# Head norm of the differential attention moved from ScalarE and VectorE to GpSimd, with a reciprocal root by Newton steps

## What is computed

```python
def diff_attention(q, k, v, lam):          # 8 heads, head width 2 * 64 = 128
    s = einsum("bqhmd,bkhmd->bhmqk", qi, k) * d ** -0.5
    p = softmax(s, axis=-1)
    a = p[:, :, 0] - lam * p[:, :, 1]
    return einsum("bhqk,bkhe->bqhe", a, v)

def rms_norm(x, g):
    return x * rsqrt(mean(x * x, axis=-1) + EPS) * g

def diff_output(o, subln_g, lam_init, w_out):
    o = rms_norm(o, subln_g) * (1.0 - lam_init)   # over the 128 values of a head
    return o.reshape(B, L, D_MODEL) @ w_out
```

## Time and profile before

| | us |
|---|---|
| median of three timed runs | 4042.5 (4040.92 to 4044.31) |
| the profiled execution, its own time | 4037.7 |
| its span, first to last instruction | 4035.9 |

### The profile page before, as it was taken

One profiled execution on the slowest core, in us unless ns is written; L12 is line 12 of the kernel. 1 busy time (PEld: TensorE's weight loads), 2 busy tenths in 40 slices (PEclk: granted clock), 3 DMA queues, 4 the chain that ended last, 5 costly groups with the idle time before them and its releaser, 6 DMA issues.

```text
span 4035.9 us, 52710 instructions
## 1 busy us (share of the span) xinstructions
PE 3755.6 (93%) x22128; PEld 2863.9 (71%) x22128; DVE 1688.5 (42%) x4142; ACT 809.4 (20%) x1872; POOL 195.6 (5%) x271
## 2 busy tenths in 40 slices
PE   6978999889997999999997999889989799999996
PEld 2435545554444999999994554777764699999996
DVE  5442002474524544444423320777752554444442
ACT  1103000121002111111112000666640211111112
POOL 0000000000000000000000000000000000000001
PEclk9998999989997999999998999999999799999998
DMA  8651011222232788888871110100011388888886
GB/s 326 242 196 62 21 48 56 82 102 104 85 134 97 258 285 284 286 284 283 284 270 64 36 42 21 45 17 17 9 74 68 118 277 284 285 282 284 285 280 220
DMA packets 280302, 655.47 MB, mean 162 GB/s; under 512 B 8808, under 2 KB 9185, under 8 KB 276802
## 3 DMA queue, kind: packets, MB, share of 16 engines
q1 hardware_dynamic: 245202, 517.05, 35.6%
q0 software_dynamic: 34864, 135.05, 10.8%
HBM read 588.76 MB, written 57.02 MB: 160 GB/s over the span
## 4 chain that ended last, share of the span: by engine, by line
PE 86%; DVE 5%; ACT 5%; DMA 2%; issue 1%; SPq 0%; POOL 0%; DVEq 0%; ACTq 0%; POOLq 0%
PE ps L1075 25%; PE ps L784 14%; PE ps L1101 12%; PE ps L956 6%; PE ps L787 6%; PE ps L753 3%; PE ps L1151 3%; PE ps L891 3%; PE ps L907 3%; PE ps L1201 2%; PE ps L1170 2%; ACT hT L1454 1%; ACT hT L1268 1%; PE ps L1106 1%; PE ps L705 1%
## 5 line engine op out<-in xcount | busy, mean ns | idle before, releaser
L1075 PE MATMUL ps<-big,ring 128*128 128x144 f32 x8192 | 1031.7, 288 | 4.2 <-DVE big L1920 4.2
L1075 PEld LDWEIGHTS ps<-big,ring 128*128 128x128 f32 x8192 | 1014.6, 191 | 13.1 <-issue 11.8
L784 PE MATMUL ps<-hT,ring 128*128 128x384 f32 x1728 | 562.3, 489 | 6.2 <-issue 6.2
L1101 PE MATMUL ps<-big,ring 128*128 128x144 f32 x4096 | 512.0, 286 | 0.0
L1101 PEld LDWEIGHTS ps<-big,ring 128*128 128x128 f32 x4096 | 505.6, 190 | 0.0
L784 PEld LDWEIGHTS ps<-hT,ring 128*128 128x128 f32 x1728 | 330.6, 191 | 237.3 <-issue 11.4
L1948 DVE TENSOR_TENSOR big<-big,ps 128x144 f32<-128x144 f32 x256 | 77.8, 304 | 502.7 <-ACT big L1398 499.3
L1398 ACT ACTIVATE big<-ps 128x144 f32<-128x144 f32 x256 | 74.3, 290 | 980.5 <-PE ps L1075 980.5
L956 PE MATMUL ps<-ring,yT 128*128 128x512 f32 x576 | 247.5, 592 | 0.0
L787 PE MATMUL ps<-ring,hT 128*128 128x512 f32 x576 | 247.5, 592 | 0.0
L1988 DVE TENSOR_REDUCE gst<-ps 128x1 f32<-128x1152 f32 x144 | 173.2, 1232 | 149.5 <-PE ps L1155 149.3
(11 more groups left out here) (343 smaller groups left out, 3839.4 us busy)
## 6 DMA issues: line engine op xcount, KB each, us to landing
ring<-in_moe_wg SPq DMA_DIRECT2D x64, 2048.0 KB, 10.4
ring<-in_moe_wu SPq DMA_DIRECT2D x64, 2048.0 KB, 13.9
ring<-in_moe_wd SPq DMA_DIRECT2D x64, 2048.0 KB, 11.3
ring<-in_w_mod SPq DMA_DIRECT2D x24, 2048.0 KB, 12.3
big<-aff_t POOLq DMA_DIRECT2D x30, 512.0 KB, 3.9
ring<-in_w_in_even SPq DMA_DIRECT2D x7, 2048.0 KB, 7.8
ring<-in_w_in_odd SPq DMA_DIRECT2D x6, 2048.0 KB, 10.0
big<-x_res POOLq DMA_DIRECT2D x24, 512.0 KB, 8.0
```

Source lines behind the costliest of these rows:

```text
L784: i = mm(ps[:, b + g, 0:384], w[:, k, c * P:(c + 1) * P], hTv[:, k, g * 384:(g + 1) * 384], start=k == 0, stop=k == DK - 1)
L1075: last_mm = mm(ps[:, 3 + f % 2, g * CAP:(g + 1) * CAP], w[u - n0][:, k, c * P:(c + 1) * P], xsT[b][:, k, :], start=k == 0, stop=k == DK - 1)
L1101: last_mm = mm(ps[:, 3 + d % 2, 0:CAP], w[4 + d // 4][:, k, (d % 4) * P:(d % 4 + 1) * P], hid[:, k, :], start=k == 0, stop=k == DK - 1)
```

## The change

The root and the scaling go to GpSimd. At q == 8 VectorE still makes the mean square, and then a first guess for the reciprocal root by shifting its bits right by one (into `gstf[:, 60:69]`); it signals `a.var` after that. GpSimd waits for `a.var`, finishes the guess with one instruction (multiply by -1, add a constant, on the bits taken as integers), makes four Newton steps of four instructions each on nine columns, and multiplies the head's 128x1152 values by the result. All 17 small instructions go through a `Chain`, each waiting for the one before. The norm of head h - 2 stands behind `swap_halves(h)` in GpSimd's queue; the last two heads' norms follow. The Sqrt on ScalarE (`deviations`) and `norm_head` on VectorE are gone. VectorE waits for the previous head's `a.on` before it overwrites the columns.

```diff
--- before.py
+++ after.py
@@ -136,7 +136,7 @@
                    "e.cbev": ("e.act_ctx", 0), "e.cxev": ("e.act_ctx", 4), "e.c0ev": ("e.act_ctx", 9),
                    "e.c1ev": ("e.act_ctx", 12), "e.coh": ("e.dve_ctx", 0), "e.xctx": ("e.dve_ctx", 2),
                    "a.kt": ("r.kt", T), "a.s": ("r.stmm", 16), "a.t": ("r.sc", T), "a.pv": ("h.x", 10),
-                   "a.ckT": ("r.ktev", T), "a.tev": ("r.oev", T), "a.e": ("h.vtev", 2 * T), "a.std": ("r.std", 1),
+                   "a.ckT": ("r.ktev", T), "a.tev": ("r.oev", T), "a.e": ("h.vtev", 2 * T),
                    "a.nm": ("r.sm", T), "a.a": ("r.qf", 8), "a.oev": ("r.on", T), "a.var": ("r.var", 1)}
 
         def common(name):
@@ -648,8 +648,27 @@
             pool.wait_ge(*at("q.ev", 34))
             pool.dma_start(out[4][0, 0].rearrange("t h d -> t (h d)"), va[:, 8, :]).then_inc(s("out"), 16)
             pool.wait_ge(*at("a.kctx_out", 16))
+            def norm_head(ch, h):
+
+                pool.wait_ge(*at("a.var", h + 1))
+                x, y, w = gstf[:, 48:57], gstf[:, 60:69], gstf[:, 72:81]
+                tt = nc.gpsimd.tensor_tensor
+                ch(nc.gpsimd.tensor_scalar(y.bitcast(I32), y.bitcast(I32), -1.0, float(0x5f3759df), ALU.mult, ALU.add))
+                for _ in range(4):
+                    ch(tt(w, y, y, ALU.mult))
+                    ch(tt(w, w, x, ALU.mult))
+                    ch(nc.gpsimd.tensor_scalar(w, w, -0.5, 1.5, ALU.mult, ALU.add))
+                    ch(tt(y, w, y, ALU.mult))
+                r = y.rearrange("p (t o) -> p t o", o=1).to_broadcast([P, T, P])
+                tt(ohs[h % 2], ohs[h % 2], r, ALU.mult).then_inc(s("a.on"), 1)
+                pool.wait_ge(*at("a.on", h + 1))
+
+            roots = Chain(pool, "pool.roots")
             for h in range(2, AH):
                 swap_halves(h)
+                norm_head(roots, h - 2)
+            for h in (AH - 2, AH - 1):
+                norm_head(roots, h)
             after_mixer(1)
             experts(1)
             ld(misc[:, 0:1024].rearrange("p (o d) -> p o d", o=1),
@@ -1461,10 +1480,6 @@
                         act.wait_ge(*at("a.t", before + g + 1))
                         A(dst(512 * g, w), ps[:, 6 + g % 2, 0:w], ACT.Copy, **kw).then_inc(s("a.tev"), 1)
 
-                def deviations(h):
-                    act.wait_ge(*at("a.var", h + 1))
-                    A(gstf[:, 48:57], gstf[:, 48:57], ACT.Sqrt).then_inc(s("a.std"), 1)
-
                 exps(0)
                 act.wait_ge(*at("a.kctx_out", 16))
                 exps(1)
@@ -1474,14 +1489,11 @@
                         act.wait_ge(*at("a.pv", n))
                     evacuate(lambda o, w: aT[:, o:o + w], done, 9 if q < 8 else 1)
                     done = tev_of[n]
-                    if q == head_step - 1 and h:
-                        deviations(h - 1)
                     if n + 2 < len(steps):
                         exps(n + 2)
                     if q == head_step and h:
                         evacuate(lambda o, w: yTv[:, h - 1, o:o + w], done, 9, scale=lamc[:, 6:7])
                         done = head_tev[h - 1]
-                deviations(AH - 1)
                 evacuate(lambda o, w: yTv[:, AH - 1, o:o + w], done, 9, scale=lamc[:, 6:7])
 
 
@@ -1988,13 +2000,6 @@
                         nc.vector.tensor_reduce(gstf[:, c + 2 + m:c + 3 + m], bank(3 * m, 3)[:, 0:w], AX.X, ALU.max,
                                                 negate=True).then_inc(s("a.nm"), 1)
 
-                def norm_head(h):
-                    dve.wait_ge(*at("a.std", h + 1))
-                    ch(rec(gstf[:, 60:69], gstf[:, 48:57]))
-                    r = gstf[:, 60:69].rearrange("p (t o) -> p t o", o=1).to_broadcast([P, T, P])
-                    tt(ohs[h % 2], ohs[h % 2], r, ALU.mult).then_inc(s("a.on"), 1)
-                    dve.wait_ge(*at("a.on", h + 1))
-
                 def mix(n):
 
                     w = NT if steps[n][1] < 8 else P
@@ -2014,8 +2019,6 @@
                         mix(n + 1)
                     if n + 2 < len(steps):
                         maxima(n + 2)
-                    if q == head_step - 1 and h:
-                        norm_head(h - 1)
                     dve.wait_ge(*at("a.pv", n + 1))
                     if q == 0 and h >= 2:
                         dve.wait_ge(*at("a.tev", head_tev[h - 2]))
@@ -2025,9 +2028,12 @@
                     dve.wait_ge(*at("a.oev", n + 1))
                     ch(stt(junk2, o[:, q, :], 1.0, o[:, q, :], ALU.mult, ALU.mult, accum_out=gstf[:, 36 + q:37 + q]))
                     if q == 8:
-                        ts(gstf[:, 48:57], gstf[:, 36:45], 1.0 / P, EPS, ALU.mult, ALU.add).then_inc(s("a.var"), 1)
+                        if h:
+                            dve.wait_ge(*at("a.on", h))
+                        ch(ts(gstf[:, 48:57], gstf[:, 36:45], 1.0 / P, EPS, ALU.mult, ALU.add))
+                        ts(gstf[:, 60:69].bitcast(I32), gstf[:, 48:57].bitcast(I32), 1, None, ALU.arith_shift_right
+                           ).then_inc(s("a.var"), 1)
                         dve.wait_ge(*at("a.var", h + 1))
-                norm_head(AH - 1)
                 dve.wait_ge(*at("a.on", AH))
                 dve.sem_inc(s("m1.big_free"), 1)
```

## The result

The changed kernel takes 4030.66 us (median of 10 runs, 4023.73 to 4036.69), the kernel before 4041.71 us (10 runs, 4036.71 to 4047.1): 11 us less, a ratio of 0.997 with a 95% interval of 0.996 to 0.9979. The forecast was 4033.4, or 9.1 us less.

What follows compares the result with a forecast made beforehand. TensorE was taken to bound the attention. ScalarE's stall gone (-22.2), a longer tail (+6.1) and VectorE waiting beside GpSimd (+7.0) gave -9.1 us, so 4042.5 would fall to 4033.4 us; range 4023 to 4050.

Steps and rivals of the forecast that it cites:

- ScalarE's stall: Heads 1 to 7, q = 0 to 2: without Sqrt and table loads the steps fall to 5.85 us, gaining 22.2 us.
- more than four head ends with a low clock: Head ends in the attention: a sign that would show the prediction wrong; no size given.
- 18.0 if clock drops only move elsewhere: Lower bound of the gain from ScalarE's removed table loads, 7 x 2.57 us, against 22.2 booked.
- VectorE's scaling "by itself worth nothing": VectorE at q = 1: its scaling lies inside ScalarE's stall, so removing it alone gains nothing.
- GpSimd's chain: Per head on GpSimd: 17 small instructions at 0.3 us, 5.1 us, then the scaling at 2.7 us.
- The slack to q = 2: Between heads: the norm is done 8.3 us after L2028 starts, leaving 10 us of slack, so no cost.
- R3: Rival, chance 0.07: at 1.1 us a link GpSimd misses the date of q = 2; +20.5 us, 4063.
- R4: Rival, chance 0.06: another wait at q = 1 replaces ScalarE's, only the tail is left; +6.1 us, 4048.6.
- The tail: Last head's norm, with nothing beside it: 8.3 us where it took 2.18, so 6.1 us more.
- VectorE beside a working GpSimd: Attention, heads' ends: VectorE waits for GpSimd's scaling, 1.0 us a head, 7.0 us lost in all.
- R2: Rival, chance 0.21: VectorE waits for the whole scaling in every head, 16.1 us, net 0; 4042.5, up to 4052.
- R1: Rival, chance 0.24: GpSimd disturbs nobody, VectorE loses nothing beside it; -16.1 us, 4026.4.

Runs made afterwards that it cites:

- e4_steps3: The changed kernel with three Newton steps on GpSimd where it has four; median 4021.61 us, ratio 0.995.
- e1_copy: The kernel before, with ScalarE's Sqrt of nine columns replaced by a Copy, so no table loads in the attention; 4025.06 us, ratio 0.9963.
- e2_scale_dve: The changed kernel with the scaling of 128x1152 back on VectorE at q = 1, the small instructions staying on GpSimd; 4029.12 us.
- the second execution: The changed kernel run and profiled once more with no edit; median 4027.94 us.
- e8_busy: The changed kernel with three Newton steps, the last head's norm back on ScalarE and VectorE, nine unread matmuls at q = 0 of heads 1 to 7; 4011.15 us.
- e3_steps5: The changed kernel with five Newton steps on GpSimd where it has four; median 4032.07 us.
- e11_busy_steps5: The kernel of e8_busy with five Newton steps where it has three; median 4012.26 us.

## Why the prediction was right

The sum said -22.2 + 6.1 + 7.0 = -9.1 us; the stretch shows -10.7 and the medians -11. The ways of the single terms are partly opposite.

- *ScalarE's stall.* Right: of the loads one is left, and q = 0, 1, 2 are 5.85 us apart where nothing meets. The load that the Sqrt behind the attention now needs lies at 3043.12, in ScalarE's idle time (the Sqrt follows at 3055.77), as forecast. The undisturbed sum of q = 0 to 3 is 135.6 (e4_steps3), 23.7 under the kernel before; the forecast had 22.2, since it left the step q = 2 to 3 at 7.89 us, and it takes 7.67.
- *The clock.* This step failed: "more than four head ends with a low clock" was one of the prediction's own signs of being wrong, and it is what the trace shows. Of the 22.2 us, 4.2 were drops at q = 1 that were booked as gained. The head ends took 4.65 us more instead: all seven now show a drop where four did, in both profiled executions; the kernel before was profiled once. The range's own bound, "18.0 if clock drops only move elsewhere", was the true case. e1_copy shows six of the seven without GpSimd.
- *VectorE's scaling "by itself worth nothing".* No run tests this under the old stall. Once that is gone it costs 0.57 us a head, 0.82 with the reciprocal (e2_scale_dve, e1_copy). This is what the move to GpSimd buys over taking away the table loads alone; the forecast's sum did not need it.
- *GpSimd's chain.* 0.3 us a link was forecast, 0.285 measured; the scaling 2.7 against 2.11. The estimate of 2.5 us worked out from the Trainium skill (GPSIMD Engine Reference, section 3.1) was nearer and still too long. The slack to q = 2 was never touched: R3 did not occur, nor did R4.
- *The tail.* +6.1 forecast, +5.36 measured (7.54 us from the mean square to the turns, a little under the 8 to 10 named as the sign); of the 0.76 us too many, some 0.5 are the scaling and the rest the chain.
- *VectorE beside a working GpSimd.* VectorE does wait for the scaling's end, as the forecast and R2 assumed, but the size was 3.0 us (138.6 - 135.6; 3.5 in the second execution) and not 7.0, nor R2's 16.1. So this wait is real, and the total still lies between the forecast and R1, not between the forecast and R2 as the prediction concluded from it: that the second engine waits does not yet say how long, and that is decided by where the scaling starts. With a drop at every head end the squares come late, 0.85 us before the scaling's end in head 2, and 0.3 of that is free. The forecast's 1.0 us a head and more appeared as soon as the phases changed (1.0 in e8_busy, 1.7 in the even heads of e3_steps5); R2's 2.3 appeared nowhere. R1, no disturbance, was reached with one Newton step less.

Together, by the sizes of these misses: -9.1 - 1.5 + 4.65 - 0.7 - 4.0 = -10.7. That the total came within 2 us is partly luck: the clock term and the term for VectorE's wait were wrong by 4.65 and 4.0 us, in opposite directions.

## What to carry to other kernels

Look first for what an instruction drags along: two table loads around a Sqrt on nine columns made nearly the whole stall, and without them (e1_copy, which leaves out the root) the attention was already 14 us shorter. The work moved to GpSimd cost nothing between the heads only where it read SBUF while VectorE did not read two operands from there; its start mattered more than its length, and with a longer chain the attention was 5.3 us shorter (e11_busy_steps5). Keep the last piece, which nothing covers, on the engines that do it soonest, and try filling TensorE's short waits when the clock falls behind them; then look again at what the faster steps bring together.

## What was not expected of the hardware

- A wait of TensorE of 2.3 to 2.5 us can be followed by a stretch at a lower mean clock (0.72 over 6 us), and then costs 1.6 us (7.8 for 6.2 us), at times 3. It was so at all seven head ends of the changed kernel, but only at four in the kernel before, and behind the 2.50 us of q = 1 only in three heads of seven; the wait before the scores was 2.31 us at the end of head 1, with a drop, and 2.32 at the end of head 2, without. Nine matmuls that nobody reads removed it at every head end of the five kernels that have them, and twelve more in the tail took 3.1 us off the way to the output projection.
- VectorE or GpSimd, waiting for the other's SBUF read, is recorded as busy: squares of 0.29 us appear as 0.37, 0.99, 1.52 or 2.19, a GpSimd multiply of 0.20 as 1.18, the scaling of 2.11 as 3.11. A group's mean hides this; for the short instructions the end gives it away, for it falls 0.06 to 0.14 us behind the other's end.
